# A two-layer streaming encoder step on one core: where a retention step's full-precision matmuls stand in its projection, and where its group statistics stand on VectorE

## What is computed

```python
mod = silu(c) @ w_ada + b_ada                 # shift, scale, gate
h = rms_norm(x, g_pre) * (1 + scale) + shift  # x: 1024 prompt rows, 64 sample rows
q_a, k_a, v_a, gate_a, q_i, k_i, w_i, q_b, k_b, v_b, gate_b = split_cols(h @ w_in)
o_a = dsa_attention(...)                      # top-256 keys by an indexer, 8 heads of 64
o_b = head_group_norm(retention(q_b, k_b, v_b, s0))   # 4 heads of 128
mixed = concat([o_a * silu(gate_a), o_b * silu(gate_b)])
x = x + gate * rms_norm(mixed @ w_out, g_post)
```

```python
att = (q @ k.T) * decay_mask
o = att @ v + (q @ s) * q_decay
s = s * s_decay + (k * k_decay).T @ v
```

## Time and profile before

| | before |
|---|---|
| median of 3 runs | 1515.44 us (1513.92 to 1519.77) |
| the profiled execution's own time | 1513.14 us |
| its span | 1511.3 us |
| TensorE busy | 1398.7 us, 93% of the span |
| VectorE busy | 1046.3 us, 69% |
| ScalarE busy | 784.6 us, 52% |
| GpSimd busy | 410.7 us, 27% |
| chain that ended last, by engine | TensorE 56%, VectorE 28%, issue 5%, ScalarE 5%, DMA 4% |
| granted TensorE clock, mean | 0.986 |

### The profile page before, as it was taken

One profiled execution on the slowest core, in us unless ns is written; L12 is line 12 of the kernel. 1 busy time (PEld: TensorE's weight loads), 2 busy tenths in 40 slices (PEclk: granted clock), 3 DMA queues, 4 the chain that ended last, 5 costly groups with the idle time before them and its releaser, 6 DMA issues.

```text
span 1511.3 us, 24328 instructions
## 1 busy us (share of the span) xinstructions
PE 1398.7 (93%) x7591; PEld 1058.8 (70%) x7591; DVE 1046.3 (69%) x3021; ACT 784.6 (52%) x1916; POOL 410.7 (27%) x360
## 2 busy tenths in 40 slices
PE   6779999999999889889996999999999988988996
PEld 2655777777887567557875577877888756755885
DVE  1697888999996456542297889999998645654224
ACT  2545665666225556554453566666622655655431
POOL 2541343334321011001287114444432101100100
PEclk9999999999999999999998999999999999999998
DMA  8412333332232102113242111121122211211324
GB/s 311 132 59 73 104 115 118 114 108 74 55 93 59 37 31 71 60 56 114 89 167 66 32 45 49 48 58 34 52 70 73 60 33 37 69 56 58 111 78 160
DMA packets 125190, 122.04 MB, mean 81 GB/s; under 512 B 33256, under 2 KB 94024, under 8 KB 125064
## 3 DMA queue, kind: packets, MB, share of 16 engines
q1 hardware_dynamic: 124608, 120.36, 25.9%
q10 hardware_dynamic: 456, 0.13, 0.0%
HBM read 93.55 MB, written 26.90 MB: 80 GB/s over the span
## 4 chain that ended last, share of the span: by engine, by line
PE 56%; DVE 28%; issue 5%; ACT 5%; DMA 4%; POOL 0%; SPq 0%; DVEq 0%; ACTq 0%; POOLq 0%
PE proj L937 11%; PE proj L938 11%; PE proj L940 10%; PE turn L916 8%; DVE U L1638 5%; PE logit L964 5%; PE out_bank L989 5%; DVE U L1828 2%; DVE by_cos_sin L1576 2%; PE spare L964 2%; DVE by_cos_sin L1578 2%; DMA U<-x_dram 1%; DVE turned L1593 1%; DVE probsT_more L1711 1%; ACT probsT_more L1275 1%
## 5 line engine op out<-in xcount | busy, mean ns | idle before, releaser
L937 PE MATMUL proj<-w_hi,h_hi 128*128 128x512 f32 (+2 forms) x1440 | 577.8, 401 | 3.6 <-POOL h_lo L1441 2.2
L938 PE MATMUL proj<-w_lo,h_hi 128*128 128x512 f32 (+2 forms) x1440 | 537.7, 373 | 0.0
L940 PE MATMUL proj<-w_hi,h_lo 128*128 128x512 f32 (+2 forms) x1280 | 479.8, 375 | 0.0
L1435 POOL TENSOR_TENSOR w_lo<-w_raw,w_hi 128x512 fp32r<-128x512 f32 (+2 forms) x160 | 206.7, 1292 | 806.9 <-ACT w_hi L1164 806.8
L937 PEld LDWEIGHTS proj<-w_hi,h_hi 128*128 128x128 f32 x1440 | 273.8, 190 | 62.9 <-issue 22.6
L938 PEld LDWEIGHTS proj<-w_lo,h_hi 128*128 128x128 f32 x1440 | 274.1, 190 | 31.0
L940 PEld LDWEIGHTS proj<-w_hi,h_lo 128*128 128x128 f32 x1280 | 242.3, 189 | 37.1
L1638 DVE TENSOR_SCALAR_CACHE_REDUCE U<-score,cand 128x384 bf16<-128x384 f32 x310 | 222.6, 752 | 2.2
L964 PE MATMUL logit<-keys,queries 64*128 64x512 f32 (+4 forms) x454 | 139.0, 550 | 20.9 <-ACT U L1295 11.0
L1275 ACT ACTIVATE probsT_more<-turn 128x512 f32<-128x512 f32 (+3 forms) x156 | 73.4, 492 | 147.5 <-PE turn L916 115.3
L1576 DVE TENSOR_TENSOR by_cos_sin<-rows,cos_b 128x256 f32<-128x256 f32 (+1 forms) x126 | 66.6, 529 | 79.5 <-ACT rows L1214 75.6
(11 more groups left out here) (184 smaller groups left out, 2123.3 us busy)
## 6 DMA issues: line engine op xcount, KB each, us to landing
w_raw<-in_w_in_dram SPq DMA_DIRECT2D x80, 256.0 KB, 3.1
probsT_more<-in_w_ada_dram SPq DMA_DIRECT2D x64, 256.0 KB, 3.6
score<-mixed_dram SPq DMA_DIRECT2D x36, 256.0 KB, 2.9
score<-in_w_ada_dram SPq DMA_DIRECT2D x32, 256.0 KB, 4.9
w_raw<-in_w_out_dram SPq DMA_DIRECT2D x32, 256.0 KB, 3.4
U<-in_x_prompt_dram SPq DMA_DIRECT2D x14, 512.0 KB, 4.0
mixed_dram<-U SPq DMA_DIRECT2D x24, 192.0 KB, 2.1
gates_dram<-U SPq DMA_DIRECT2D x18, 256.0 KB, 2.2
```

The lines of the kernel that those rows point to most:

```text
L937: nc.tensor.matmul(out, h_hi[:, k, tile], hi, start=(k == 0), stop=False)
L938: ins = nc.tensor.matmul(out, h_hi[:, k, tile], lo, start=False, stop=(t == SAMPLE and k == KT - 1))
L940: ins = nc.tensor.matmul(out, h_lo[:, k, tile], hi, start=False, stop=(k == KT - 1))
L1435: nc.gpsimd.tensor_tensor(w_lo[:, s % WS, 0:w], w_raw[:, n % RAWS, 0:w], w_hi[:, s % WS, 0:w].bitcast(F32), ALU.subtract).then_inc(w_lo_re ...
```

## The change

It moves three things and leaves every instruction as it is. The retained products and ada's matmuls go from the second quarter to the third (`TURN_QUARTER`), the output products from the first to the third, behind the retained ones and ahead of the turn; ScalarE's copy of the output goes with them. On VectorE `measure_retained` goes behind the second half of the counting passes (and so behind `sum_sample`).

```diff
@@ plan_units
-            if kind(j) == "ret" and q == 1:
+            if kind(j) == "ret" and q == TURN_QUARTER:
                 logits += [("att", j), ("kv", j)]
@@ TensorE, middle
-                if kind(g) == "ret" and q == 1:
+                if kind(g) == "ret" and q == TURN_QUARTER:
                     turns.wait_taken(pe, ("q", g))
@@ TensorE, loop
-                    if q == 1:
+                    if q == TURN_QUARTER:
                         for a in ada_slices(i + 1):
                             pe.wait_ge(more_landed[a % ADA_SLOTS], 16 * (a // ADA_SLOTS + 1))
...
-                    if q == 0:
+                    middle(i - 1, q)
+                    if q == TURN_QUARTER:
                         late(i - 2)
-                    middle(i - 1, q)
@@ ScalarE, loop
                     if q == 0:
-                        late(i - 2)
                         if 0 <= i < STEPS and tested_bit(i) is not None:
                             test_bit(i)
                     middle(i - 1, q)
+                    if q == TURN_QUARTER:
+                        late(i - 2)
                     if q == TURN_QUARTER and kind(i) in ("idx", "ret", "att"):
                         take_turn(i)
@@ VectorE, loop
-                    if q == 2 and kind(i - 2) == "ret":
-                        measure_retained(i - 2)
                 if i + 1 < STEPS and lct(i + 1)[2] == SAMPLE:
                     sum_sample(i + 1)
                 for n in passes_here[half:]:
                     count_pass(n)
+                if kind(i - 2) == "ret":
+                    measure_retained(i - 2)
```

## The result

The changed kernel takes 1525.87 us in the median of 4 runs (1525.33 to 1526.21), the kernel before beside it 1516.70 (4 runs): a ratio of 1.0069, with a 95% interval of 1.0054 to 1.0083. It is slower, and by more than 0.5%. Forecast was 1519.0, no difference that can be told. Against the profiled execution of before (span 1511.3) the span is 1523.5: 12.2 us more, where I had added 3.6.

The account below looks back on a forecast made before the run. TensorE's throughput was taken to bound the kernel, alternating with VectorE near the sample tile. Profiled 1513.1 - 2.4 for breaks + 6 for VectorE's losses gave 1516.7; the median's 2.3 above the profiled run made 1519 us, range 1510 to 1527.

Parts of the forecast that it names:

- P: Time into a retention step when VectorE starts the bit's settling; the root was to start at P + 0.17 us.
- the slower rival's harder form: GpSimd's root also holds VectorE's settling; twelve events lose 1.0 us more each, giving 1531 us; chance 0.06.
- Layer 1 loses about 0.4 + 2.1 + 1.4 + 1.5 = 5.4 us: Layer 1's retention: late splits delay rope in four kinds of steps, 5.4 us together.
- the four steps like 906.70: Layer 1 retention steps where rope ends 5.10 instead of 4.08 us in; 0.14 us lost, about 0.4 together.
- the third steps of the heads: Layer 1 retention: late rope delays the turn by 0.3, 0.9 and 0.9 us, none in the first head.
- the four sample steps: Layer 1 retention: step 925.07 has rope 0.9 us later, the others lose 0 to 0.35; 1.4 for all.
- the four short steps: Layer 1 sample-tile steps of 16 matmuls can't absorb a delay: 0.7 to 0.8 us in two, 1.5 in the sum.
- the slower rival's milder form: Only the carry-over of delays into the following steps is larger than forecast: 1524 to 1527 us; chance 0.16.
- VectorE then waits some 0.3 us in 16 steps: Steps with a modulation group: products start 1.3 us later; VectorE's wait is covered by its later wait for the port.
- its 0.3 us costs nothing: ScalarE's output copy, moved behind the two sign tests, fits its idle time ahead of the turn's copy.
- 0.035 a step: TensorE's gain from removing two of three breaks per retention step, over some 70 steps: 2.4 us.
- the faster rival: Breaks cost more than read and VectorE's losses don't come: 1509 to 1513 us; chance 0.17.

Follow-up runs that it names:

- e9: The kernel before with one wait added on GpSimd, so the split behind every third tile runs after the bit's settling: 1524.07 us, ratio 1.0059.
- e2: The kernel before with only the statistics moved behind the second half of the counting passes: 1525.78 us, ratio 1.0054.
- e4: The kernel before with only GpSimd's order changed, the root one iteration later and behind that iteration's split: 1513.79 us, ratio 0.9984.
- e1: The changed kernel with the statistics back in their old place, so the regrouping alone: 1515.75 us, ratio 0.9993.
- e5: e1 with the retained and output products back in their old quarters in the gate chunk's steps: 1513.45 us, ratio 0.9988.
- e6: e5 with GpSimd's root one iteration later, behind that iteration's split: 1509.79 us, ratio 0.9957.
- e12: e6 run again without an edit, against the kernel before: 1510.07 us, ratio 0.9962.
- e3: The changed kernel with GpSimd's root one iteration later, behind that iteration's split: 1520.17 us, ratio 1.0019.

## Why the prediction was wrong

**Right.** The mechanism of the loss: late mean, late root, late split, long rope sum. For the step 1006.86 I had rope's end at 5.69 us into the step; it is 1018.49 + 1.29 less 1014.02, 5.76. I had 0.9 lost there, and it is 1.03. Some luck is in that: the settling starts 3.20 us into the step rather than 2.93, and rope ends 2.56 behind it rather than 2.76. The root starts at P + 0.16 (1017.38 against 1017.22; I had 0.17) and does not hold VectorE's settling, which takes 0.21 and 0.23 beside it, nor rope's first product, 0.42. So the slower rival's harder form (root and settling together, 1531) is out, and here the rows show what the earlier trace rows could not: the VectorE instruction there, L1652, reads a single tile, so it says nothing of instructions with two inputs. The Trainium skill's GPSIMD Engine Reference (8. Key points) has GpSimd contend with VectorE's instructions that have two SBUF inputs; the split's rows bear that out, the root's beside rope's first product (0.42 us) don't. I had counted the root's own inputs; the ones that count there are VectorE's. e9 shows that a late split, with the gating behind it, is enough for most of the loss; e2 that the statistics' move alone makes all of it in this stage.

**Wrong, the size of it: "Layer 1 loses about 0.4 + 2.1 + 1.4 + 1.5 = 5.4 us".** Against it stood 36 x 0.035 = 1.3 of gain, so +4.1 net; measured is +7.45. e2 is the cleaner measure of the loss, since it has neither the gain nor a fall of the clock in this stage: +7.34. From the starts of the steps, each against before:

| steps of layer 1 | predicted loss | e2 | changed kernel, gain included |
|---|---|---|---|
| the four steps like 906.70 | 0.4 | 0.06 | 0.13 |
| the third steps of the heads | 2.1 | 1.84 | 1.46 |
| the four sample steps | 1.4 | 1.08 | 2.37 |
| the four short steps | 1.5 | 1.84 | 1.91 |
| all others | 0 | 2.52 | 1.58 |

The sum over the steps that I had priced is 4.8 in e2 against 5.4: that part was right, if a little high. The step that failed is the last row, a term put at nothing: steps in which the event lay one or more steps back. They cost 2.5 us in e2. (In the changed kernel the two steps around 937 us, with the fall of the clock in them, are 1.91 us longer than before together; in e2 the same two are 0.08 longer.) The largest piece that both traces have is the step from 1102.44, 7.94 us where 6.63 stood, and the changed kernel's rows say why:

```profile
1102.17 0.79 POOL L1463 TENSOR_SCALAR U<-U,probs_last,rstd 128x128 f32<-128x128 f32 x1
...
1103.05 1.01 POOL L1467 TENSOR_TENSOR U<-U 128x384 f32<-128x384 f32 x1
...
1103.42 0.67 DVE L1653 TENSOR_SCALAR rej<-cnt 128x5 int32<-128x5 f32 x1
1104.02 1.28 POOL L1436 TENSOR_TENSOR w_lo<-w_raw,w_hi 128x512 fp32r<-128x512 f32 x1
1104.12 1.20 DVE L1656 SCALAR_TENSOR_TENSOR cand<-rej,cand 128x5 int32<-128x5 int32 x1
```

A late split pushes GpSimd's three normalizing instructions and the gating into the next step, where the gating and the next split run back to back; VectorE's two small instructions, 0.17 us each where nothing meets them, take 0.67 and 1.20. I followed the split to its first victim and did not follow GpSimd's queue any further, though I had named the case (the slower rival's milder form, 1524 to 1527) and given it 0.16. That was too little: the profile before already has a gating that holds such an instruction for 1.00 us (at 932.80, shown with e4), and I did not look for it.

**Wrong, the terms at nothing: "VectorE then waits some 0.3 us in 16 steps" and "its 0.3 us costs nothing".** Both were worked out for retention steps, where VectorE's later wait for GpSimd's split or TensorE's own time covers them. The last two retention steps' products fall into gate steps, where VectorE is the limit and nothing covers a wait. I had no term for them; measured is +1.65 for both chunks (e1: 0.96 and 0.82, e5: 0.21 and 0.02), of which the waiting itself, 0.16 and 0.45 us in layer 0, is a part. In the earlier trace rows the gate step stands with VectorE busy 5.30 of 5.44; I read TensorE's 5.44 in that row and not the other number.

**A little low: "0.035 a step".** It is 0.053. I took two thirds of the 0.05 that 0.456 us for two products and 0.23 for the turn had left over. Means over 15 undisturbed steps of before show the parts: each group of products adds 0.46 us, the turn 0.25, and another 0.02 lies in slightly long pitches of the next step's first quarter, which I had not counted. A single group adds 1.14 in all. The time of the faster rival, 1509 to 1513, exists as a kernel, e6 and e12, but not by that rival's mechanism alone: it took the old quarters in the gate steps and the root behind the split.

**Not predicted, and not traced to the change: the indexer chunks, +3.08 us in the profiled executions.** No instruction of them was moved. TensorE's granted clock falls to half (1.2 GHz) for a short stretch in 8 places before and in 12 after. Three of the four new places are in these chunks, one (937) is in layer 1's retention. The windows of one and the same indexer step, the kernel before and then the changed one:

```profile
816.27:824.03 7.76, 4.95 (x38) 4.68 (x37) 5.59 (x14) 2.55 (x7) 4.39 (x4) 1.00 0.26 60
```

```profile
818.50:827.80 9.30, 6.53 (x39) 6.22 (x36) 5.63 (x14) 3.00 (x8) 4.41 (x5) 0.82 0.28 67
```

The granted clock is 0.82 in the second, and it is 1.5 us longer. Among the repeated runs of the kernel before, the spread is 1512.57 to 1523.12, so such falls come and go without any change. That they are the change's doing is not borne out by the other runs: layer 0's indexer chunk takes 88.74 us in the changed kernel, but 91.19 in e4, 90.18 in e12 and 88.80 in e6, all three faster than before, and 87.11 in e2, which is slower. In medians, the measured loss is 9.2 us, and the retention and gate stages (7.45 - 0.44 + 1.65) give 8.7, with the fall at 937 us in it.

**The chances.** The sum stood 3.5 us above no change, and the measurable limit at 7.6. For the loss alone I had bounds of 0 and 14 around a sum of 6, so 4 us more of it were well inside them. 0.20 for slower was too little for that.

## What to carry to other kernels

An instruction that moves inside one engine's order can cost nothing there and still be dear, when an in-order queue on another engine waits for it: write down what stands behind the waiter, when each of those now runs, and what it runs beside, until the queue is idle again, not only to the first collision. Price a delay in each kind of step separately, the last steps of a stage included: their late work falls into the next stage, which can have another limit. And where a shared resource couples two engines, choose the order by which of the queued instructions does harm: here the big split goes first and the small root behind it. Such a repair wants a control without the fault beside it (e4), since it can be worth something by itself, and then a look at which steps it changed.

## What the runs showed of the hardware

- A GpSimd instruction with two large inputs in SBUF (split 128x512, gating 128x384) holds even VectorE instructions on five columns, one of them (L1653) with a single tile as input: 0.17 us becomes 0.67, 1.00, 1.14 and 1.20. The root (three columns) and the normalizing tensor-scalar of GpSimd run beside rope's products without touching them (0.42 and 0.46 in e6), though beside the gate chunk's mask instructions the root itself took 1.52 us in e3. A counting pass is not held: one of 512 columns took 0.74 us in the changed kernel with a split beginning beside it (1090.40 and 1090.63), and 0.74 with none (1105.89).
- The price of breaking the fp32r projection for full-precision matmuls isn't the same for each break: 0.040 us for the first that is joined to another, 0.013 for the second. The full-precision products themselves follow each other 0.22 us apart in a group of two as in one of five.
- A change of order by 0.4% was told apart here with 6 and 12 runs beside 30 and 23 of the kernel before. One kernel's time spreads over 10 us in 29 runs, and the clock has its part in that: 1516.98 to 1520.01 us where the mean granted clock was 0.980, 1512.57 and 1515.11 where it was 0.987.
